# Layer four of a four-layer network: small VectorE work moved to GpSimd, and four queues reordered

## What is computed

```python
def mla_mixer(h, positions, w_in, q_norm_g, kv_norm_g, w_q_up, w_kv_up, qn_g, kn_g):
    z = h @ w_in                                  # q 512 | kv 256 | k_rope 64 | q_mem 512
    cq  = rms_norm_2(z[..., :512], q_norm_g)
    ckv = rms_norm_2(z[..., 512:768], kv_norm_g)
    q  = (cq @ w_q_up).reshape(b, s, 8, 192)      # 128 without rope, 64 with
    kv = (ckv @ w_kv_up).reshape(b, s, 8, 256)    # 128 k, 128 v
    k  = concat([kv[..., :128], k_rope broadcast to 8 heads])
    q, k = rms_norm_2(q, qn_g), rms_norm_2(k, kn_g)
    q, k = rope on the last 64 of each, by positions
    return causal_block_attention(q, k, v), q_mem

x = x + concat([mix, memory_attention(q_mem, mem_k, mem_v)]) @ w_out
x = x + hierarchical_moe(rms_norm_2(x, norm2_g), ...)
```

## Time and profile before

| | us |
|---|---|
| median of 3 runs | 1565.11 (1561.64 to 1566.87) |
| the profiled execution | 1564.71 |
| its span, first to last instruction | 1562.9 |
| TensorE busy in the span | 1491.0 (95%) |
| VectorE busy | 1318.1 (84%) |
| ScalarE busy | 1044.5 (67%) |
| GpSimd busy | 117.9 (8%) |
| layer four's mixer | about 1108 to 1250 of the span |

### The profile page before, as it was taken

The page is one execution under the profiler, slowest core; times in us unless marked ns, Lnnn a source line. Parts: engine busy times, 40 slices in busy tenths (PEclk is TensorE's granted clock), DMA queues, the critical chain, the costliest instruction groups (busy, mean ns, idle before and its releaser), DMA issues.

```text
span 1562.9 us, 21164 instructions
## 1 busy us (share of the span) xinstructions
PE 1491.0 (95%) x7102; PEld 1220.2 (78%) x7102; DVE 1318.1 (84%) x1989; ACT 1044.5 (67%) x1533; POOL 117.9 (8%) x215
## 2 busy tenths in 40 slices
PE   8999999979999999999989999999898979999998
PEld 5887877857878778778767888888787768888886
DVE  6778899887878999877678899989886789999897
ACT  4555677744646677657457777777586657777775
POOL 4030000030207000020120000000000000000000
PEclk9999999989999999999989999999999989999999
DMA  8435699975537899864548999999542439999996
GB/s 313 153 117 175 206 336 346 326 226 173 170 109 233 288 342 329 289 206 137 153 131 294 360 356 361 360 340 356 191 161 82 151 108 360 359 361 359 358 332 224
DMA packets 307903, 399.74 MB, mean 256 GB/s; under 512 B 16956, under 2 KB 221500, under 8 KB 307540
## 3 DMA queue, kind: packets, MB, share of 16 engines
q1 hardware_dynamic: 298500, 382.00, 73.7%
q0 software_dynamic: 9296, 16.39, 3.6%
HBM read 397.28 MB, written 1.05 MB: 255 GB/s over the span
## 4 chain that ended last, share of the span: by engine, by line
PE 75%; DVE 19%; ACT 3%; issue 2%; DMA 0%; DVEq 0%; ACTq 0%; POOLq 0%
PE bank L662 21%; PE bank L663 21%; PE bank L664 21%; DVE w_lo_at L2085 6%; PE bank L822 2%; PE bank L679 1%; PE bank L849 1%; PE bank L991 1%; ACT w_hi_at L1480 1%; DVE t_lo_at L2107 1%; DVE uc_at L2690 1%; PE bank L796 1%; PE bank L797 1%; ACT probs_a_at L1719 0%; DVE x_at L2517 0%
## 5 line engine op out<-in xcount | busy, mean ns | idle before, releaser
L2085 DVE TENSOR_TENSOR w_lo_at<-raw_at,w_hi_at 128x1024 fp32r<-128x1024 f32 (+1 forms) x730 | 853.9, 1212 | 88.4 <-ACT w_hi_at L1480 75.1
L1480 ACT ACTIVATE w_hi_at<-raw_at 128x1024 fp32r<-128x1024 f32 (+1 forms) x730 | 726.1, 1046 | 139.6 <-PE bank L664 73.5
L662 PE MATMUL bank<-w_hi_at,xs_hi_at 128*128 128x512 f32 x800 | 324.1, 405 | 3.3 <-DVE xs_lo_at L2509 1.6
L664 PE MATMUL bank<-w_hi_at,xs_lo_at 128*128 128x512 f32 x800 | 314.6, 393 | 0.0
L663 PE MATMUL bank<-w_lo_at,xs_hi_at 128*128 128x512 f32 x800 | 314.5, 393 | 0.0
L662 PE MATMUL bank<-w_hi_at,t_hi_at 128*128 128x512 f32 (+3 forms) x528 | 210.4, 399 | 13.8 <-DVE w_lo_at L2085 3.9
L664 PE MATMUL bank<-w_hi_at,t_lo_at 128*128 128x512 f32 (+3 forms) x528 | 203.0, 384 | 0.0
L663 PE MATMUL bank<-w_lo_at,t_hi_at 128*128 128x512 f32 (+3 forms) x528 | 202.9, 384 | 0.0
L662 PEld LDWEIGHTS bank<-w_hi_at,xs_hi_at 128*128 128x128 f32 x800 | 151.1, 189 | 35.8 <-issue 2.5
L664 PEld LDWEIGHTS bank<-w_hi_at,xs_lo_at 128*128 128x128 f32 x800 | 150.8, 189 | 34.5
L663 PEld LDWEIGHTS bank<-w_lo_at,xs_hi_at 128*128 128x128 f32 x800 | 151.4, 189 | 29.3
(11 more groups left out here) (521 smaller groups left out, 1692.4 us busy)
## 6 DMA issues: line engine op xcount, KB each, us to landing
raw_at<-in_moe_w_dram SPq DMA_DIRECT2D x192, 512.0 KB, 5.5
raw_at<-in_moe_w_gate_dram SPq DMA_DIRECT2D x128, 512.0 KB, 6.0
raw_at<-in_moe_w_up_dram SPq DMA_DIRECT2D x128, 512.0 KB, 7.5
raw_at<-in_moe_w_down_dram SPq DMA_DIRECT2D x128, 512.0 KB, 6.2
raw_at<-in_w_in_dram SPq DMA_DIRECT2D x40, 512.0 KB, 4.9
raw_at<-in_a_w_in_dram SPq DMA_DIRECT2D x20, 512.0 KB, 4.7
raw_at<-in_w_out_dram SPq DMA_DIRECT2D x16, 512.0 KB, 4.6
raw_at<-in_ple_wg_dram SPq DMA_DIRECT2D x16, 512.0 KB, 5.3
```

The costliest lines, as they stand in the source:

```text
L662: pe.matmul(out, ah, bh, start=start, stop=False, skip_group_check=loose)
L664: return pe.matmul(out, al, bh, start=False, stop=stop, skip_group_check=loose)
L1480: act.activation(WH[:, s.part(), a], RAW[:, s.slot(), a], ACT.Copy).then_inc(hi_half[i], 1)
L2085: dve.tensor_tensor(WL[:, s.part(), a], RAW[:, s.slot(), a], WH[:, s.part(), a].bitcast(F32), ALU.subtract).then_inc(split_half[i], 1)
```

## The change

Six things, all in layer four:

1. `angles` moves from VectorE to GpSimd. A scaled addition in one instruction becomes a product and an addition, so 26 chained instructions replace 20, with a cast and two products ahead of them. It starts when the last output of layer three's experts has been added.
2. The split of Q2 stands ahead of `stats` on VectorE; on both engines the next split (M1) moves behind the root of `ckv`, and on ScalarE ahead of the sine.
3. `KRP`, the rope part of the keys, moves to GpSimd (`turned_key_heads`), which waits for a new signal, `k_root`. VectorE waits for `k_rope` before it uses the root's buffer again.
4. `rotate(0)` and `rotate(1)` move to GpSimd, behind `turned_key_heads`.
5. ScalarE copies the memory probabilities out ahead of `query_block(1)` instead of behind `query_squares(1)`.
6. TensorE multiplies the memory heads ahead of turning the keys; `k_nope` takes banks 5, 7, 2, 3 instead of 5, 7, 4, 6, and the rotated queries of the first half are turned in the middle of query unit 3. The queues of ScalarE and VectorE follow this.

```diff
 # GpSimd, behind low_tokens(2)
+            def angles():
+                pool.wait_ge(*params_in["cols2"].at(0))
+                pool.wait_ge(*dve_ready.at(("moe_out", 2)))
+                ch.do(pool.tensor_copy(POSF[:, :], POS[:, :]))
+                for tb in range(TB):
+                    ch.go(pool.tensor_scalar(TRIG[:, 4, tb, :], INVF, POSF[:, tb:tb + 1], None, ALU.mult))
+                ch.sync()
+                a, k, t = TRIG[:, 4, :, :], TRIG[:, 5, :, :], TRIG[:, 1, :, :]
+                for dst, shift in ((TRIG[:, 2, :, :], 0.25), (TRIG[:, 3, :, :], 0.0)):
+                    ch.do(pool.tensor_scalar(k, a, 1.0 / TWO_PI, shift, ALU.mult, ALU.add))
+                    ch.do(pool.tensor_scalar(k, k, ROUND, None, ALU.add))
+                    ch.do(pool.tensor_scalar(k, k, -ROUND, None, ALU.add))
+                    ch.do(pool.tensor_scalar(t, k, -TURN1, None, ALU.mult))
+                    ch.do(pool.tensor_tensor(dst, t, a, ALU.add))
...
+                pool.nop().then_inc(*pool_ready.tick("angles"))
+            def turned_key_heads():
+                pool.wait_ge(*dve_ready.at("k_root"))
+                for tb in range(TB):
+                    rb = RS[:, 8 * tb:8 * tb + 8].unsqueeze(2)
+                    ch.go(pool.tensor_tensor(KRP[:, tb, :].rearrange("p (h c) -> p h c", c=64),
+                                             KRG[:, tb, :].unsqueeze(1).to_broadcast([P, 8, 64]), rb.to_broadcast([P, 8, 64]),
+                                             ALU.mult))
+                ch.sync()
+                pool.nop().then_inc(*pool_ready.tick("k_rope"))
+            turned_key_heads()
+            rotate(0)
+            rotate(1)
 # TensorE
             unit_q(2)
-            turn("k_nope", lambda h: KV[:, :, 256 * h:256 * h + P], 8, [dve_ready.at("k")], low=False, banks=(5, 7, 4, 6))
             mem_values(3, ("heads_m", 3), ATC, (4, 6))
-            turn("k_rope", KRP, 4, [], low=False, banks=(5, 7))
+            turn("k_nope", lambda h: KV[:, :, 256 * h:256 * h + P], 8, [dve_ready.at("k")], low=False, banks=(5, 7, 2, 3))
+            turn("k_rope", KRP, 4, [pool_ready.at("k_rope")], low=False, banks=(5, 7))
...
-            turn_queries(0, (5, 7, 4))
-            unit_q(3)
+            turn_query_heads(0, (4, 6))
+            unit_q(3, lambda: turn_rotated(0, 5))
 # ScalarE
             act.activation(ZB[:, 0, 512:832], BK[0][:, 0:320], ACT.Copy, scale=RSM[:, 0:1]).then_inc(*evac_a.tick("z_kv"))
-            split()
...
             root("ckv", 2)
-            act.wait_ge(*dve_ready.at("angles"))
+            split()
+            act.wait_ge(*pool_ready.at("angles"))
...
             query_squares(0)
+            mem_probs_t(3, 0, ATC, (4, 5))
+            mem_probs_t(3, 1, ATC, (6, 7))
             query_block(1)
             query_squares(1)
-            mem_probs_t(3, 0, ATC, (4, 5))
-            mem_probs_t(3, 1, ATC, (6, 7))
+            turn(("heads_m", 3), 4, TH[:, 4:8, :], banks=(4, 6))
+            turn("k_nope", 8, KTN, banks=(5, 7, 2, 3), scale=GNK[:, 2:3])
+            turn("k_rope", 4, KTR, banks=(5, 7))
             query_block(2)
-            turn("k_nope", 8, KTN, banks=(5, 7, 4, 6), scale=GNK[:, 2:3])
-            turn(("heads_m", 3), 4, TH[:, 4:8, :], banks=(4, 6))
-            turn("k_rope", 4, KTR, banks=(5, 7))
+            turn(("q_nope", 0), 4, QTN[:, 0:4, :], banks=(4, 6))
             query_squares(2)
-            split()
-            turn_queries(0, (5, 7, 4))
+            turn(("q_rope", 0), 2, QTR[:, 0:2, :], banks=(5,))
+            split()
             query_block(3)
 # VectorE
             split(4 * 320)
             split()
+            split()
             stats(0)
             stats(1)
...
-            angles()
-            split()
             used(first, 1)
             dve.tensor_scalar(ZB[:, 1, 512:832], BK[1][:, 0:320], RSM[:, 1:2], None, ALU.mult).then_inc(*evac_d.tick("z_kv"))
-            split()
...
             done("ckv")
+            split()
...
             rooted("k", 16)
+            done("k_root")
...
             query_squares(0)
+            query_block(1)
             split(4 * 384)
-            query_block(1)
             query_squares(1)
-            rotate(0)
+            turn(("heads_m", 3), 4, TH[:, 4:8, :], TL[:, 4:8, :], banks=(4, 6))
             query_block(2)
-            turn(("heads_m", 3), 4, TH[:, 4:8, :], TL[:, 4:8, :], banks=(4, 6))
             query_squares(2)
             split()
             query_block(3)
             query_squares(3)
+            dve.wait_ge(*pool_ready.at("k_rope"))
```

More of the change, by code:

```diff
@@ new lines, in _ @@
+            angles()
+            def turned_key_heads():
[7 more added lines that the diff above has]
+                pool.nop().then_inc(*pool_ready.tick("k_rope"))
@@ new lines, in rotate @@
+            def rotate(half):
+                pool.wait_ge(*evac_a.at(("q_up", 2 * half + 1)))
+                pool.wait_ge(*evac_d.at(("q_up", 2 * half + 1)))
+                x_ = QQ[:, :, 768 * half:768 * half + 768].rearrange("p b (h c) -> p b h c", c=192)[:, :, :, P:192]
+                o_ = QRP[:, :, 256 * half:256 * half + 256].rearrange("p b (h c) -> p b h c", c=64)
+                t_ = [SROW[:, 256 * i:256 * i + 256].rearrange("p (b h c) -> p b h c", b=TB, c=32) for i in range(2)]
+                q_ = [QTAB[:, i, :, :].unsqueeze(2).to_broadcast([P, TB, 4, 32]) for i in range(4)]
+                x1, x2, o1, o2 = x_[:, :, :, 0:32], x_[:, :, :, 32:64], o_[:, :, :, 0:32], o_[:, :, :, 32:64]
+                for o, a, b in ((o1, x1, q_[0]), (t_[0], x2, q_[1]), (o2, x1, q_[2]), (t_[1], x2, q_[3])):
+                    ch.go(pool.tensor_tensor(o, a, b, ALU.mult))
+                ch.sync()
+                ch.go(pool.tensor_tensor(o1, o1, t_[0], ALU.subtract))
+                ch.go(pool.tensor_tensor(o2, o2, t_[1], ALU.add))
+                ch.sync()
+                pool.nop().then_inc(*pool_ready.tick(("rotated", half)))
@@ L3159, in _ @@
             weigh(1)
-            rotate(1)
             split()
```

58 lines of the change are left out of this document (18 added, 40 removed).

## The result

| | before | with the change |
|---|---|---|
| median | 1565.84 (13 runs) | 1557.93 (13 runs) |
| lowest to highest | 1559.63 to 1568.83 | 1552.01 to 1560.09 |
| ratio | | 0.9948, 95% interval 0.9935 to 0.9962 |
| the profiled execution | 1564.71 | 1556.73 |
| its span | 1562.9 | 1554.9 |

The change makes the kernel faster by 0.5%, and the interval stays clear of no change. Forecast were 1558.0 and a range of 1554.8 to 1563.5. In the table of experiments further down, one execution of e1 (2659.82 us) and one of before beside the last group (3277.03 us) were far slower than the rest; the medians count them, the ratios do not.

What follows compares the result with a forecast made beforehand. TensorE, busy 95% of 1562.9 us, bounds the kernel; time returns only where it waits or runs slowly. -3.3 + 0.2 - 5.7 + 1.2 + 0.6 = -7.0 from 1564.71 gives 1557.7, said as 1558; range 1554.8 to 1563.5.

Steps and rivals of the forecast that it cites:

- Q2's wait, -3.3: Early mixer: splitting Q2 ahead of the statistics removes TensorE's wait for its low halves, 3.3 us gained.
- +0.2 for the port: Early mixer: GpSimd's new work delays VectorE's splits at the shared SBUF port, at most 0.2 us lost.
- The GpSimd chain: Angles as 28 steps of at most 0.56 us, 15.7, plus 2.5 waiting for VectorE; hidden, 1.2 us to spare.
- Part two, -5.7: Earlier probability copy and heads ahead of keys remove waits of 3.71 and 0.39 and 1.6 of slow clock.
- part one: Mixer start: Q2's split ahead of the statistics and angles on GpSimd; 3.3 us gained, at most 0.2 lost.
- Given back, +1.2 for the late query block 3: Before the attention weights: last query sum only 4.3 us earlier, not 5.7; with 0.2 slack, 1.2 us lost.
- Port on the chain to the weights, +0.6: Last query sum to attention weights: a VectorE split waits for one GpSimd rotation operation, 0.6 us lost.
- The port eats part two: Rival: second-half rotations hold VectorE once per operation, 4.2 us on the chain to the weights; 1561.3 us, chance 0.19.
- Part two does nothing: Rival: the keys' signal, not bank 5, caused the 3.71 us wait ahead of k_nope; 1561.6 us, chance 0.07.
- Late angles: Rival: GpSimd steps above 0.8 us make TensorE wait for M2, one for one; 1572 at 1.3 us, chance 0.07.
- Nothing given back: Rival: ScalarE's slack covers the late output split ahead of query block 3; 1555.9 us or less, chance 0.08.
- the waits alternate: Argument against the 4.2 us port loss: GpSimd and VectorE would hold each other up in turn at the port.

Runs made afterwards that it cites:

- e1: Kernel before with only the angles on GpSimd and the mixer's first three queues as in the change; stretch 134.28 us against 137.92, ratio 0.9979.
- e10: e3 with the angles also on VectorE, behind its half of the kv block; stretch 132.29 us, median 1560.32, ratio 0.9957.
- e4: The change with ScalarE copying the memory probabilities behind the squares of query block 1 again; stretch 135.93 us against 130.19, ratio 0.9996.
- e8: The change with the k_nope transposes ahead of the memory heads again, banks kept; stretch 132.67 us, one run, 1555.12.
- e3: The change with rope keys and both rotations back on VectorE; stretch 129.23 us, median 1556.3, ratio 0.9944.
- e7: The change with 24 more chained GpSimd steps behind the angles; stretch 142.79 us, median 1571.01, ratio 1.002.
- e9: The change with rope keys and rotations on VectorE and query block 3 ahead of the first output split; stretch 128.93 us, median 1554.97, ratio 0.9914.
- e12: The kernel of e2 run again; stretch 135.41 us, one run, 1563.21.
- e2: The change with the angles back on VectorE and the first queues in the old order; stretch 135.43 us, median 1562.36, ratio 0.9976.
- e14: The kernel of e5 run again; stretch 130.55 us, one run, 1560.2.
- e5: The change with query block 3 and its squares ahead of the first output split on ScalarE and VectorE; stretch 132.13 us, ratio 0.9948.
- e13: The change itself run again; stretch 131.79 us against 130.19, one run, 1559.01.

## Why the prediction was right, step by step

- **Q2's wait, -3.3, and +0.2 for the port.** Measured -3.64 (e1), and no port cost. The 3.33 in brackets is not quite what is lost: it begins at the modelled end of the last pass, while the next pass would have started 0.16 sooner, and the first two passes behind it stand 0.34 and 0.24 apart instead of 0.23. 3.33 + 0.16 + 0.12 is 3.6. TensorE held behind Q2 too, as said; e10 shows how little room there is, since 5 us more on VectorE gave 2.75 of waits.
- **The GpSimd chain.** 0.56 a step was the upper end; without the two held steps they take 0.43 each on average, 12.1 instead of 15.7. The 2.5 us for waiting behind VectorE's six passes were too little: one GpSimd step was held over all six, 5.9 us more than usual, and the last one, beside a seventh pass, 0.9 more, which is 6.8 in all. The two errors cancel, and that was luck: the chain took 18.95 us, from 1107.12 to 1126.07, and 15.7 + 2.5 = 18.2 was said. Hidden, with 0.1 us of room on ScalarE, where 1.2 was said, and 3.7 us on TensorE.
- **Part two, -5.7.** TensorE now comes for the attention weights at 1197.01 - 2.14 = 1194.87, 85.95 into the stretch, before 95.92. Less part one that is 6.3. The extra 0.6 are mostly the slow clock, whose price was set too low: the sixteen transposes held TensorE for 3.72 us until the next instruction began (1179.36 to 1183.08), and now for 1.75 (1173.70 to 1175.45), so 2.0 and not 1.6 went. The wait itself was 0.16 longer than its bracket, as at Q2. The 0.5 that the prediction names for ScalarE freeing banks 5 and 7 behind the heads is in none of its sums (1179.3 + 2.1 + 1.0 + 1.0 + 0.5 would be 1183.9, not 1183.5), and it didn't come: `k_nope` ran through in 1.91. That the late copy held TensorE is shown by e4 and e8. That it did so through bank 5 is read from the trace of before: the copies of banks 4 and 5 ended at 1179.21, and TensorE began at 1179.36. No run changes the banks alone.
- **Given back, +1.2 for the late query block 3.** The last sum came 5.0 us sooner (85.71 to 77.07, less 3.64), TensorE 6.3; less the slack of 0.2 that leaves 1.1. As said, though both numbers were larger than said.
- **Port on the chain to the weights, +0.6.** It was 1.0 (e3): 0.6 on the split, 0.4 on the small product, which I hadn't counted since it has one input. So 2.1 given back instead of 1.8.
- **Sum:** -3.6 - 6.3 + 1.1 + 1.0 = -7.8, measured -7.73, said -7.0. That the median of 1557.93 lies 0.1 from the 1558 is luck. The forecast started from 1565.11, the median of three runs, and over 13 runs before has 1565.84; the gain in the medians is 7.9 and not 7.1, and the two differences cancel. And the change has a wait after which half clock comes in some executions, for 1.6 us; the profiled one had none.
- **Rivals.** "The port eats part two" was right in kind and wrong in size, 1.0 instead of 4.2: of six operations of GpSimd most fell beside a reduction or idle time of VectorE, and only two spots met, the small product and the split. "Part two does nothing" fell with e4. "Late angles" is real but 3.8 us away (e7). "Nothing given back" is what e9 comes near to.

The lock of the Trainium skill, SBUF — State Buffer, "Who interferes with whom", is borne out in kind by the held 6.26 us and by the small product: the page lists `tensor_scalar` among the operations that can take the shared pair. The 7 us that the prediction worked out by this rule for the chain were nearer than its 2.5: the two held steps cost 6.8. What the page says of the order, for VectorE's two-port modes ("Whoever issues first gets the shared pair for the whole instruction"), doesn't lead one to expect that a queue of passes keeps the other engine out between them, and the trace shows that it did so with one step.

## What to carry to other kernels

Before moving small work to another engine, reorder the queues: of the 7.7 us, 5.7 came from order (0.6 at the start, 5.1 from the memory attention on), 3.1 from the angles' move, and the rope's move took 1.0 back (e10 has the order alone, at 132.29). Move only what stands in front of someone's need and has nobody waiting for it itself, and look for two-input SBUF passes on the other side of the port at both its old and its new time. When a wait's named releaser had been done for microseconds, look at who last owned the bank, and test by moving the line that frees it.

## What was unexpected of the hardware

- **The same wait is followed by half clock in some executions and not in others.** After 3.3 us ahead of Q2: granted clock 1.00 before and in e12, 0.69 and 0.50 in e2. After 2.0 to 2.2 us ahead of the attention weights: 1.00 in the change, e2, e4 and e14; 0.50 to 0.8 in e5, e7, e8, e12 and e13. The longer waits, 3.71 (before and e1), 3.91 (e4) and 7.99 (e7), were each followed by it, in one trace each. After the waits of 2.0 to 3.3 us it costs 1.6 us each time, more than many a change is worth. None of the traces shows it after the waits of 0.85 and 1.15. The Trainium skill, TensorE: Matmul & The Clock Gate, "What's actually happening", says this of the slow passes at a kernel's start: how many there are varies from run to run of one kernel. The traces show the like behind waits in the middle of one. In the 13 runs of the change the mean granted clock of 0.989 goes with the two fastest (1552.01 and 1552.99), and 0.982 or 0.983 with the six slowest, from 1558.93 on.
- **Back-to-back VectorE passes can keep GpSimd out.** One step, a `tensor_scalar` of 64 elements, was held over six split passes, 6.24 to 6.27 us in every trace that has the angles on GpSimd; VectorE was not slowed. It isn't always so. Operations of GpSimd with two inputs got in behind one pass each, and then VectorE's next pass was held in its turn: in e5 two of them took 1.60 and 1.72 us instead of 0.73 inside VectorE's queue of four, and the queue took 6.01 instead of 4.63. So "the waits alternate" of the prediction holds for these and failed for the one step. The two differ in their number of inputs, but no run tests that this is why. Two key products on VectorE took 4.10 us beside GpSimd's two rope products, and twice 1.23 in the kernel before with GpSimd idle, as the timeline of VectorE and of GpSimd in the change shows:

```profile
1165.41 4.10 DVE L3135 TENSOR_TENSOR kv_at<-kv_at,rs_at 128x1024 f32<-128x1024 f32 x2 [0.18 <-DVE rs_at L2250]
```

```profile
1165.40 3.03 POOL L677 TENSOR_TENSOR krp_at<-krg_at,rs_at 128x512 f32<-128x512 f32 x2 [39.32 <-DVEq L2142]
```

- **An instruction of VectorE with one input was held too**: 128x16 in 0.58 us (0.48 in e5) instead of 0.17, beside GpSimd's products.

What stays open: why one execution drops the clock and the next doesn't, and where the 1.34 us behind the mixer went; nothing was changed there, and the same part of the kernel took 314.4 to 316.6 us over the traces of kernels that leave it as it is (317.2 in e7).
